# Two products of a transformer kernel fed with unscaled activations to their end, and the split of later weights placed between a scaling and the convolution's taps

## The reference, cut to what matters

```python
# first network, second half
h = h + conv_ffn(rmsnorm(h, norm_ffn_g), w_up, conv_w, conv_b, w_down)

def conv_ffn(xn, w_up, conv_w, conv_b, w_down):
    h = xn @ w_up                                    # 1024 -> 5632
    h = causal_depthwise_conv3(h, conv_w) + conv_b   # over the tokens, 3 taps
    a, b = jnp.split(h, 2, axis=-1)
    return (jax.nn.silu(a) * b) @ w_down

# second network, last half of its last layer ("w1_1" and "w2_1" in the kernel)
x = x + gate * (jnp.square(jax.nn.relu(modulated @ w1)) @ w2)        # 1024 -> 4096 -> 1024
# modulated = rms(x) * g * (1 + scale) + shift
```

## Time and profile before

| | |
|---|---|
| median of 3 runs | 1425.15 us (1420.35 to 1425.94) |
| the profiled execution | 1423.98 us, of which the span from its first to its last instruction is 1422.2 us |
| PE, PE's weight loads | busy 1366.4 us (96%), 1158.2 us (81%) |
| DVE, ACT, POOL | busy 714.1 us (50%), 604.7 us (43%), 448.6 us (32%) |
| transfers | 220.14 MB, mean 155 GB/s |
| w_up on PE | from 249.5 to 395.7 us of the span |
| w1_1 on PE | from 1225.6 to 1327.1 us of the span |

### The profile page before, as it was taken

One profiled execution on the slowest core, in us unless ns is written; L12 is line 12 of the kernel. 1 busy time (PEld: TensorE's weight loads), 2 busy tenths in 40 slices (PEclk: granted clock), 3 DMA queues, 4 the chain that ended last, 5 costly groups with the idle time before them and its releaser, 6 DMA issues.

```text
span 1422.2 us, 20872 instructions
## 1 busy us (share of the span) xinstructions
PE 1366.4 (96%) x8436; PEld 1158.2 (81%) x8436; DVE 714.1 (50%) x1129; ACT 604.7 (43%) x997; POOL 448.6 (32%) x440
## 2 busy tenths in 40 slices
PE   7889999999999999998999999999899999899999
PEld 7777788789999677875788888888577777799999
DVE  7575447757765635227122232222657766844443
ACT  6334445556664322225332133322445544665432
POOL 4532121333342000314440024401266643477200
PEclk9999999999999999999999999999999999999999
DMA  7346567686555445245533332323522221455552
GB/s 279 118 167 206 194 228 242 216 299 234 178 178 179 180 166 173 87 137 184 172 100 93 100 100 93 103 90 104 207 97 96 79 101 45 163 166 187 182 182 85
DMA packets 63968, 220.14 MB, mean 155 GB/s; under 512 B 6912, under 2 KB 10240, under 8 KB 63872
## 3 DMA queue, kind: packets, MB, share of 16 engines
q1 hardware_dynamic: 63584, 218.56, 46.2%
q10 hardware_dynamic: 288, 0.25, 0.1%
HBM read 217.73 MB, written 1.05 MB: 154 GB/s over the span
## 4 chain that ended last, share of the span: by engine, by line
PE 80%; DVE 9%; POOL 4%; ACT 3%; issue 2%; DMA 1%; SPq 0%; DVEq 0%; POOLq 0%; ACTq 0%
PE ps L476 23%; PE ps L490 22%; PE ps L488 22%; PE ps L532 3%; DVE wlo L1419 2%; PE ps L795 1%; POOL tmp L2144 1%; PE ps L822 1%; PE ps L742 1%; PE ps L809 1%; DVE tmp L1685 1%; DVE tmp L1687 1%; DVE Alo L1832 1%; PE ps L483 1%; PE ps L788 1%
## 5 line engine op out<-in xcount | busy, mean ns | idle before, releaser
L476 PE MATMUL ps<-Ahi,whi 128*128 128x256 f32 (+1 forms) x1656 | 552.6, 334 | 16.6 <-ACT Ahi L942 7.0
L490 PE MATMUL ps<-Ahi,wlo 128*128 128x256 f32 (+1 forms) x1584 | 509.2, 321 | 2.2 <-DVE wlo L1419 2.2
L488 PE MATMUL ps<-Alo,whi 128*128 128x256 f32 (+1 forms) x1584 | 509.4, 322 | 0.7 <-DVE Alo L1433 0.5
L1419 DVE TENSOR_TENSOR wlo<-raw,whi 128x1024 fp32r<-128x1024 f32 x298 | 373.3, 1261 | 226.6 <-ACT whi L913 226.5
L913 ACT ACTIVATE whi<-raw 128x1024 fp32r<-128x1024 f32 x305 | 320.2, 1052 | 263.9 <-PE ps L490 217.5
L476 PEld LDWEIGHTS ps<-Ahi,whi 128*128 128x128 f32 x1656 | 319.4, 193 | 93.8 <-issue 40.8
L490 PEld LDWEIGHTS ps<-Ahi,wlo 128*128 128x128 f32 x1584 | 305.2, 193 | 24.8 <-DVE wlo L1419 3.3
L488 PEld LDWEIGHTS ps<-Alo,whi 128*128 128x128 f32 x1584 | 305.4, 193 | 23.6 <-issue 1.9
L488 PE MATMUL ps<-Hlo,whi 128*128 128x256 f32 (+2 forms) x752 | 240.0, 319 | 0.4 <-DVE Hlo L1433 0.4
L476 PE MATMUL ps<-Hhi,whi 128*128 128x256 f32 (+2 forms) x712 | 229.0, 322 | 0.0
L490 PE MATMUL ps<-Hhi,wlo 128*128 128x256 f32 (+2 forms) x712 | 228.6, 321 | 0.0
(11 more groups left out here) (257 smaller groups left out, 1244.9 us busy)
## 6 DMA issues: line engine op xcount, KB each, us to landing
raw<-in_ada SPq DMA_DIRECT2D x96, 512.0 KB, 3.6
raw<-in_w SPq DMA_DIRECT2D x64, 512.0 KB, 3.5
raw<-in_w_up SPq DMA_DIRECT2D x44, 512.0 KB, 4.4
raw<-in_w_in SPq DMA_DIRECT2D x38, 512.0 KB, 4.5
raw<-in_w_0a SPq DMA_DIRECT2D x32, 512.0 KB, 3.5
raw<-in_w_0b SPq DMA_DIRECT2D x32, 512.0 KB, 3.5
raw<-in_na_in SPq DMA_DIRECT2D x24, 512.0 KB, 6.0
raw<-in_w_down SPq DMA_DIRECT2D x22, 512.0 KB, 3.5
```

The lines of the kernel that those rows point to most:

```text
L476: e.matmul(o, w_hi, ah, start=k == 0, stop=False)
L488: e.matmul(o, w_hi, al, start=False, stop=False)
L490: m = e.matmul(o, w_lo, ah, start=False, stop=last)
L1419: e.tensor_tensor(wlo[i % NRAW][:, :cols], raw[i % NRAW][:, :cols], plain(whi[s % NHI][:, :cols]), SUB).then_inc(S("wlo").sem, 1)
```

## The change

w_up and w1_1 take the unscaled activations in all their chunks. The scaled activations (n1, m1) are no longer made. Every product of the two is scaled by `rescaled` into Y, and what follows reads Y. DVE's order in w_up becomes, at each chunk i: the low part of unit i + 2, the two taps of chunk i - 1, the scaling of product i. ACT does its part of chunk i before it finishes chunk i - 1 (SiLU or Hhi), where it finished first before. A bank is free after the scaling. POOL makes no low part in either product; DVE makes these five as well. All of w1_1's matmuls have 258 columns; its unscaled activations move from the tiles Hhi and Hlo, which the hidden values now need whole, to Ahi and Alo. No chunk of the two has the other order of matmuls.

```diff
-EARLY = {"w_in": 3, "w_up": 4, "w1_1": 3}
+EARLY = {"w_in": 3, "w_up": 44, "w1_1": 32}
...
-LOW_BY_POOL = [SPLIT_AT[key] for key in (("w_in", 2), ("w_in", 3), ("w_up", 2), ("w_up", 3), ("w1_1", 2), ("w1_1", 3),
-                                         ("w1_1", 4))]
+LOW_BY_POOL = [SPLIT_AT[key] for key in (("w_in", 2), ("w_in", 3))]
...
-    Ehi, Elo = [x[:, 8192 - 8 * 258:].rearrange("p (c t) -> p c t", c=8) for x in (Hhi, Hlo)]
+    Ehi, Elo = [x.rearrange("p c t -> p (c t)")[:, :8 * 258].rearrange("p (c t) -> p c t", c=8) for x in (Ahi, Alo)]
...
-            early = EARLY.get(name, 0)
+            early = EARLY.get(name, 0) if first else 0
...
-                    if kt == 8 and n == early:
+                    if kt == 8 and n == early and name not in ("w_up", "w1_1"):
...
-        linear("w_up", 256, lambda k: (Ahi[:, k], Alo[:, k]), ready("n1_hi"), ready("n1_lo"), during=during_up,
-               following=lambda u: ada_following("w_up", u),
-               first=(256, lambda k: (E_hi[:, k], E_lo[:, k]), ready("e1_hi"), ready("e1_lo")))
+        linear("w_up", 256, lambda k: (E_hi[:, k], E_lo[:, k]), ready("e1_hi"), ready("e1_lo"), during=during_up,
+               following=lambda u: ada_following("w_up", u))
...
-        linear("w1_1", 256, lambda k: (Ahi[:, k], Alo[:, k]), ready("m1_hi"), ready("m1_lo"), during=during_1,
-               first=(258, lambda k: (Ehi[:, k], Elo[:, k]), e2_hi, e2_lo))
+        linear("w1_1", 258, lambda k: (Ehi[:, k], Elo[:, k]), e2_hi, e2_lo, during=during_1)
...
# ACT, w_up
-                    for c in range(3):
-                        normed_hi("n1", c, n1_x[c % 3][:, :256], param("g_ffn", c))
...
-                if n >= 3:
-                    up_finish(n - 1)
-                if n < 4:
-                    w.wait_ge(S("resc_w_up"), n + 1)
-                    o = Y[n][:, :256]
-                else:
-                    o = product("w_up", n)[:, :256]
+                w.wait_ge(S("resc_w_up"), n + 1)
+                o = Y[n % 4][:, :256]
...
                 e.activation(tmp[n % 4][:, :256], o, ACT.Identity, scale=param("conv_w", 88 + ch),
                              bias=param("conv_b", ch)).then_inc(S("up_x").sem, 1)
+                if n:
+                    up_finish(n - 1)
...
# ACT, w1_1
-                    relu_up("r1", product("w1_1", n)[:, :256], tmp[n % 5][:, :256])
+                w.wait_ge(S("resc_w1_1"), n + 1)
+                if n >= 5:
+                    w.wait_ge(S("h1_lo"), n - 4)
+                relu_up("r1", Y[n % 4][:, :256], tmp[n % 5][:, :256], shift_out[:, n % 2:n % 2 + 1])
...
# DVE, w_up
+        def up_taps(n):
+            o, x = Y[n % 4][:, :256], tmp[n % 4][:, :256]
+            ch = n // 2 + 22 * (n % 2)
+            w.wait_ge(S("resc_w_up"), n + 1)
+            w.wait_ge(S("up_x"), n + 1)
+            e.scalar_tensor_tensor(x[:, 1:256], o[:, 0:255], param("conv_w", 44 + ch), x[:, 1:256], MUL, ADD).then_inc(own.sem, own.up())
+            w.wait_ge(own, own.n)
+            e.scalar_tensor_tensor(x[:, 2:256], o[:, 0:254], param("conv_w", ch), x[:, 2:256], MUL, ADD).then_inc(S("up_conv").sem, 1)
...
                 los(UNIT["w_up", i])
+                if i:
+                    up_taps(i - 1)
...
-                    norm1_steps(*((0, 3), (3, 6), (6, 10), (0, 0))[n])
...
+                if i >= 4:
+                    w.wait_ge(S("up_conv"), i - 3)
+                rescaled("n1", "w_up", i, rst[:, LEFT])
...
# DVE, w1_1
-                    m1_steps(*((0, 4), (4, 10), (0, 0))[n])
+                o = product("w1_1", n)
+                if n >= 2:
+                    w.wait_ge(S("r1"), n - 1)
+                e.tensor_copy(shift_out[:, n % 2:n % 2 + 1], o[:, 256:257]).then_inc(own.sem, own.up())
+                rescaled("m1", "w1_1", n, rst[:, LEFT])
...
# POOL
-        low("w_up", 2)
-        low("w_up", 3)
...
-        for u in (2, 3, 4):
-            low("w1_1", u)
```

More of the change, by code:

```diff
@@ L1373, in scalar_program @@
                     after_na_out(7)
[L1374 to L1379, removed]
         for what, i in walk("w1_1"):
@@ L1388, in scalar_program @@
                     root("m1", rst[:, LEFT])
[L1389 to L1395, removed]
-                    hidden_hi("h1", n - 1, 256)
[L1397 to L1402, removed]
-                    relu_up("r1", product("w1_1", n)[:, :256], tmp[n % 5][:, :256])
+                else:
+                    hidden_hi("h1", n - 1, 256)
+                w.wait_ge(S("resc_w1_1"), n + 1)
+                if n >= 5:
+                    w.wait_ge(S("h1_lo"), n - 4)
+                relu_up("r1", Y[n % 4][:, :256], tmp[n % 5][:, :256], shift_out[:, n % 2:n % 2 + 1])
         hidden_hi("h1", 31, 256)
@@ L1456, in rescaled @@
             w.wait_ge(S(st + "_r"), 1)
[L1457 removed]
+            e.tensor_tensor(Y[n % 4][:, :256], o[:, :256], r, MUL).then_inc(S("resc_" + name).sem, 1)
         def ada_copied(quad):
@@ L1669, in vector_program @@
                 los(UNIT["w_up", i])
+                if i:
+                    up_taps(i - 1)
             if what == "chunk":
-                n = i
-                written("w_up", n)
-                if n == 0:
+                written("w_up", i)
+                if i == 0:
                     mean_inverse("n1", rst[:, LEFT], ps[4][:, :256])
-                if n < 4:
-                    rescaled("n1", "w_up", n, rst[:, LEFT])
-                    norm1_steps(*((0, 3), (3, 6), (6, 10), (0, 0))[n])
-                    w.wait_ge(S("resc_w_up"), n + 1)
-                    o = Y[n][:, :256]
-                else:
-                    o = product("w_up", n)[:, :256]
-                x = tmp[n % 4][:, :256]
-                ch = n // 2 + 22 * (n % 2)
-                w.wait_ge(S("up_x"), n + 1)
-                e.scalar_tensor_tensor(x[:, 1:256], o[:, 0:255], param("conv_w", 44 + ch), x[:, 1:256], MUL, ADD).then_inc(own.sem, own.up())
-                w.wait_ge(own, own.n)
-                e.scalar_tensor_tensor(x[:, 2:256], o[:, 0:254], param("conv_w", ch), x[:, 2:256], MUL, ADD).then_inc(S("up_conv").sem, 1)
+                if i >= 4:
+                    w.wait_ge(S("up_conv"), i - 3)
+                rescaled("n1", "w_up", i, rst[:, LEFT])
             if what == "ada":
                 ada_place(i)
+        up_taps(43)
         w.wait_ge(S("gain2"), 2)
@@ L2001, in vector_program @@
                     early_lo("e2", Ehi, Elo, 7, LEFT, G[:, 1, 1, 0, 7:8])
-        m1_x = [tmp[5], X[0], X[1]]
-        def m1_lo(c):
-            w.wait_ge(S("m1_hi"), c + 1)
-            w.wait_ge(S("m1_t"), c + 1)
-            e.scalar_tensor_tensor(Alo[:, c, LEFT], m1_x[c % 3][:, :256], ada[:, 1, 0, 24 + c:25 + c], plain(Ahi[:, c, LEFT]),
-                                   ADD, SUB).then_inc(S("m1_lo").sem, 1)
-        def m1_steps(first, upto):
-            for c in range(first, upto):
-                if c < 8:
-                    if c >= 3:
-                        w.wait_ge(S("m1_lo"), c - 2)
-                    w.wait_ge(S("m1_r"), 1)
-                    e.scalar_tensor_tensor(m1_x[c % 3][:, :256], R[:, c, LEFT], G[:, 1, 1, 0, c:c + 1], rst[:, LEFT],
-                                           MUL, MUL).then_inc(S("m1_t").sem, 1)
-                if c >= 2:
-                    m1_lo(c - 2)
         for what, i in walk("w1_1"):
@@ L2027, in vector_program @@
                     mean_inverse("m1", rst[:, LEFT], ps[4][:, :256])
-                if n < 3:
-                    o = product("w1_1", n)
-                    if n == 2:
-                        w.wait_ge(S("r1"), 1)
-                    e.tensor_copy(shift_out[:, n % 2:n % 2 + 1], o[:, 256:257]).then_inc(own.sem, own.up())
-                    rescaled("m1", "w1_1", n, rst[:, LEFT])
-                    m1_steps(*((0, 4), (4, 10), (0, 0))[n])
+                o = product("w1_1", n)
[3 more added lines that the diff above has]
+                rescaled("m1", "w1_1", n, rst[:, LEFT])
         for what, i in walk("w2_1"):
```

11 lines of the change are left out of this document (1 added, 10 removed), and 6 rows, old and new, of the table IN_TURN.

## The result

The changed kernel takes 1411.92 us, median of 5 runs (1408.37 to 1413.29), against 1422.82 us (5 runs, 1419.50 to 1425.94) for the kernel before: ratio 0.992, interval 0.9895 to 0.9945. Run again in five rounds (`after_again`) it took 1410.36 against 1422.44 us: 0.9909, 0.9886 to 0.9931. That is faster by 11 to 12 us. The forecast was 1409 us (1404 to 1415.5), from a sum of 15.3 us.

The account below looks back on a forecast made before the run. PE was taken as the bound, four fifths of the chain of waits. Gains 6.25 + 0.71 + 8.32 = 15.28 us, added costs 0, gave 1408.7 from the profiled 1423.98 and 1409.9 from the median; forecast 1409 us, range 1404 to 1415.5.

Parts of the forecast that it names:

- The two stalls: PE's waits and slow clock at the starts of w_up and w1_1 go: 6.25 + 0.71 us and 8.32 us.
- 258 columns: Matmuls with 258 columns in 29 more chunks of w1_1 keep the pace of 256: cost 0, bound 0.2 us.
- ACT's order: ACT doing this chunk before finishing the last takes POOL's wait from in front of the tap's first step: cost 0.
- transfers: DMA issues move ahead with PE and ask no more than a full-pace period: cost 0; if late, at most 7 us.
- POOL's low parts: Five low parts at the two starts go to DVE, 1.22 us each, filling its waits: cost 0.
- DVE against POOL: Shared SBUF port makes DVE's pair of w_up chunks 5.9 us, 1.5 us late at the end; cost 0 to 3.5, taken 0.
- the slower rival: DVE becomes the bound in w_up, 8.14 us per pair, 35.4 us lost, 1444 us; decides from 7.2 us per pair; chance 0.04.
- Excess: 13.19 - 6.94 = 6.25 us: At w_up's chunk 4, a stretch of 13.19 us against a full period of 6.94; all 6.25 us counted as gained.
- a late DVE: Rival: POOL holds DVE up beyond its lead, or transfers are late; 3.5 to 7 us back, 1412 to 1416; chance 0.09.
- a late tap delays POOL and Hhi, Hlo, which only w_down reads: In w_up, DVE's late taps put off POOL and the hidden values that only w_down reads; listed under DVE waits, no price.
- a stall stays and the clock falls behind it: Rival: one start keeps a stall of 1 us or more with slow clock; 3 to 4 us back, 1412 to 1413; chance 0.14.
- after either start or elsewhere: Sign against the prediction: a slow clock showing up after w_up's or w1_1's start, or elsewhere; no size given.

Follow-up runs that it names:

- scaled_twice: Changed kernel with each product of w_up scaled twice by DVE into the same Y: 1419.54 us, 0.9973 of the kernel before.
- low_behind_taps: Changed kernel, but DVE makes unit i + 2's low part in w_up after the taps of chunk i - 1: 1426.93 us, 1.003 of the kernel before.
- up_only: Kernel before with the change in w_up alone, w1_1 left as it was: 1420.57 us, 0.9981 of the kernel before.
- w1_1_only: Kernel before with the change in w1_1 alone, w_up left as it was: 1414.48 us, 0.9946 of the kernel before.
- padded: Changed kernel with 59 unneeded matmuls (7.1 us) on PE between w_up and w_down: 1417.56 us, 0.9956 of the kernel before.
- pool_lows: Changed kernel, but POOL makes the five low parts of w_up and w1_1 as before: 1411.99 us, 0.9921 of the kernel before.
- scaled_in_psum: Changed kernel, but w_up's scaled products go to PSUM and not to Y in SBUF: 1410.43 us, 0.9913 of the kernel before.
- scaled_in_psum_twice: Changed kernel with each product of w_up scaled twice and its scaled products in PSUM: 1412.94 us, 0.9907 of the kernel before.
- before_again: The kernel before, unchanged, run and profiled a second time: 1425.4 us.
- before_third: The kernel before, unchanged, run again for a third profile: 1425.4 us.
- after: First profile of the whole changed kernel against the kernel before: median 1411.92 us, ratio 0.992; the profiled execution took 1412.72 us.
- up_only_again: The change in w_up alone run once more, w1_1 as in the kernel before: 1420.18 us, 0.9963 of the kernel before.

## Why the prediction was right, and where its sum was too large

**The two stalls.** Right, in place and in size within the products: 7.06 us measured for 6.25 + 0.71, 8.64 us for 8.32. PE's idle time in both is gone. The low activations at the two starts take 0.48 and 0.49 us.

**258 columns, ACT's order, transfers, POOL's low parts, all costed at 0.** Right: w1_1 lasts 92.81 us with its sum of squares (93.13 by 92.16 + 0.97), and with a DMA share of 0.92 in 263.22 to 270.16 PE still does its period in 6.94 us.

**DVE against POOL.** The mechanism was right, the size too large: forecast 5.9 us per pair, measured 5.76 less the 0.20 to 0.26 that DVE idles, 5.5 us. DVE therefore isn't late at all, where 1.5 us had been given. POOL's product takes 0.73 us, not the listed 1.59, as the argument against the slower rival had it. The Trainium skill, "SBUF — State Buffer", section "Who interferes with whom", says that a VectorE instruction with two SBUF inputs and a GpSimd instruction that reads SBUF exclude each other. The traces agree: the same tap beside POOL's Hlo takes 0.96 us with its operand in SBUF and 0.48 with it in PSUM. The rival that ends slower needed 7.2 us per pair; `scaled_twice`, with 6.1 (17 chunks in 52.00 us), is still faster than before.

**What came out too large.** 15.3 us were summed; the medians give 10.9 and 12.1 us, the mean spans over all executions 13.4. The step that was sized too large is "Excess: 13.19 - 6.94 = 6.25 us" with the sum made from it, which takes every microsecond of a stall with slow clock for recoverable, and puts nothing behind w_up. The same step for w1_1 (8.32 us) held: 8.0 us by medians. Two things were wrong for w_up.

That the result still lies in the range is luck in part. The range's upper end was given for a kept stall and a late DVE, and neither came; it covered a smaller gain of w_up instead.

First, w_up's slow clock doesn't go with its stall. The table has all executions of each kernel whose clock is on record: their number, the mean span, the mean time at the lower level, worked out as 2 x (1 - mean granted clock) x span, and the difference to before at equal slow time with its 95% interval. It uses one slope for all kernels, 0.22 ± 0.02 us of span for each us at the lower level (fitted; what is left scatters by 0.8 us; most kernels alone give 0.16 to 0.29, `low_behind_taps` 0.42).

| kernel | executions | span, us | at lower level, us | difference at equal slow time, us |
|---|---|---|---|---|
| before | 57 | 1421.9 | 33 | 0 |
| whole change | 11 | 1408.5 | 25 | -11.7 ± 0.6 |
| `up_only` | 19 | 1418.5 | 38 | -4.6 ± 0.4 |
| `w1_1_only` | 8 | 1413.1 | 26 | -7.2 ± 0.6 |
| `padded` | 7 | 1415.3 | 25 | -4.7 ± 0.7 |
| `pool_lows` | 4 | 1409.4 | 25 | -10.8 ± 0.9 |
| `scaled_in_psum` | 6 | 1408.9 | 25 | -11.3 ± 0.7 |
| `scaled_in_psum_twice` | 4 | 1410.0 | 30 | -11.2 ± 0.9 |
| `scaled_twice` | 10 | 1417.1 | 30 | -4.2 ± 0.6 |
| `low_behind_taps` | 10 | 1425.8 | 34 | +3.7 ± 0.6 |

Without w_up's stall the slow time isn't less (38 ± 4 against 33 ± 2 us). Without both stalls it is 8 us less (25 ± 5); without w1_1's alone 7 us less, but with an interval of ± 8, so that w1_1's stall takes its slow time with it is likely and not shown by `w1_1_only` alone. The two halves add up: -4.6 - 7.2 = -11.8.

Second, two waits of PE behind w_up are longer. PE in the changed kernel:

```profile
404.43 0.70 PE L561 MATMUL ps<-ssum_c,con 128*128 128x256 f32 x2 [1.07 <-POOL ssum_c L2005]
...
461.50 0.47 PE L475 MATMUL ps<-Ahi,whi 128*128 128x512 f32 x1 [1.74 <-ACT Ahi L1159]
```

and the same two in the kernel before:

```profile
410.80 0.70 PE L562 MATMUL ps<-ssum_c,con 128*128 128x256 f32 x2 [0.56 <-POOL ssum_c L2066]
...
467.49 0.47 PE L476 MATMUL ps<-Ahi,whi 128*128 128x512 f32 x1 [1.38 <-ACT Ahi L1177]
```

That is 0.51 + 0.36 = 0.9 us in this pair of profiles. Over the profiles the first wait differs less. With the old w_up it is 0.56, 0.89, 0.89 and 0.59 us (`before`, `before_again`, `before_third`, `w1_1_only`), with the new one 1.07, 1.03, 1.09 and 1.11 (`after`, `after_again`, `up_only`, `up_only_again`), 0.35 more in the mean. The second is 1.37 to 1.38 and 1.72 to 1.74 us in the same profiles, 0.36 more: together 0.7.

The first wait is w_up's tail. The last Hhi begins 4.43 us after w_up's end (393.23) where it began 3.91 after (399.59), and POOL's sums for the next norm stand behind the last Hlo. In `padded`, where the tail has 7 us more time, the wait is nearly gone. The prediction named the later Hhi ("a late tap delays POOL and Hhi, Hlo, which only w_down reads") and gave it no price, as it looked only at w_down's own matmuls. The second wait isn't the tail: `padded` has its longer form in full, and `pool_lows`, with the new w_up and its tail, has the old one. PE in `padded`, then in `pool_lows`:

```profile
409.74 0.70 PE L561 MATMUL ps<-ssum_c,con 128*128 128x256 f32 x2 [0.19 <-POOL ssum_c L2008]
...
466.79 0.47 PE L475 MATMUL ps<-Ahi,whi 128*128 128x512 f32 x1 [1.72 <-ACT Ahi L1162]
```

```profile
460.34 0.47 PE L476 MATMUL ps<-Ahi,whi 128*128 128x512 f32 x1 [1.36 <-ACT Ahi L1160]
```

`scaled_twice` and `scaled_in_psum_twice`, which also have the new w_up, show 1.37 too. The wait takes one of two lengths, 1.36 to 1.38 or 1.72 to 1.74 us, and keeps it in every profile of one kernel. What decides between them is open.

With these the account closes. w_up: 5.02 at full clock, plus 0.46 for its chunk 0 in `before_third`, less 0.7, makes 4.8; measured 4.6 ± 0.4 less at equal slow time. w1_1: 8.64 in the profile, less 0.22 x 6.8 = 1.5 for the 6.8 us at the lower level there, makes 7.1; measured 7.2 ± 0.6 less. Both comparisons use the fitted 0.22 and are no experiments of their own. The rest of the mean gain of 13.4 us in span is 0.22 x 8 = 1.7 us of slow time saved. Of the profiled execution's 15.70 us, 0.9 went to the two waits, and the 3 that are left are put down to a slow clock behind three stalls that the change doesn't touch (its last three stretches above). It spends some 20 us at the lower level there, for which 0.22 would say 4.5; the fit is a mean over many executions.

The rival "a stall stays and the clock falls behind it" was wrong in its place: no stall stays in either product. That the first median, 1411.92 us, lies close to this rival's 1412 to 1413 is no evidence for it. It also called the time at the lower level dear, which 0.22 us for each us is not. What the prediction named last as a sign against itself, a slow clock "after either start or elsewhere", did show up elsewhere, at the price of some 3 us in the profiled execution, which the range had room for.

**Open.** Why w1_1's stall, once gone, seems to take its slow time with it and w_up's does not, and what makes the second wait behind w_up longer. In the profiles here where w_up's stall had a slow clock behind it, 0 to 6.8 us at the lower level lie between 400 and 1215 us; in those without, 3.4 to 20. That fits a slow clock that comes at a later stall when it did not come at this one, but it is a comparison of a few profiles and not an experiment; `padded` speaks only against the place of the later stages. No run made a stall of a chosen length in w_up without the change.

## What to carry to other kernels

Put independent work on an in-order engine into the wait between two dependent steps of a chain: the low part between scaling and taps or behind the taps is 16 us apart with the same instructions. When a stall with slow clock behind it is to go, work out its price with and without the slow clock, and look in several executions for whether the slow clock is always there: w_up's stall gave back less than its price at full clock, w1_1's the whole with slow clock. A contention that lengthens an engine's instructions costs nothing while that engine still waits once per period, so compare its work with the period before working around it; and follow a later end of a stage's tail to whoever reads it, not only to the next stage.

## What the runs showed of the hardware that was not expected

TensorE's clock falls to the lower level behind different stalls in executions of the same kernel: w_up's stall drew 6.8 us of it in two profiles of before and none in the third, which had the same time within 1.5 us. And it is cheap: over all the executions in the table a microsecond at the lower level costs 0.22 us of span. PE's waits in w_up's stall (0.80 and 1.06 us at full clock, 0.52 and none at the lower) say why at that place; elsewhere it is not shown.

In the rows above POOL is held up by less than DVE is, though DVE's instructions stand back to back: its Hlo starts at 370.43, before the low part's end (370.66), and takes 0.83 us for 0.74, while DVE's tap behind it takes 0.96 for 0.48.
